# A zeroed tile multiplied with itself from the start of a two-block transformer kernel, and one modulation chunk moved behind the root

## What is computed

```python
c_act = jax.nn.silu(c)
for l in range(DEPTH):
    mod = c_act @ w_ada[l] + b_ada[l]
    sh1, sc1, g1, sh2, sc2, g2, sh3, sc3, g3 = jnp.split(mod, N_MOD, axis=-1)
    x = x + 0.5 * g1[:, None, :] * swiglu(modulate(x, sh1, sc1), ffn1_gate[l], ffn1_up[l], ffn1_down[l])
```

## Time and profile before

| | |
|---|---|
| median of 3 runs | 2202.4 us (2200.0 to 2204.21) |
| the profiled execution | 2208.11 us |
| its span, first to last instruction | 2206.3 us |
| mean granted TensorE clock over the span | 0.987 |
| TensorE busy | 2143.5 us, 97% |
| VectorE busy | 1525.2 us, 69% |
| ScalarE busy | 1170.7 us, 53% |
| HBM read | 418.81 MB |

### The profile page before, as it was taken

One profiled execution on the slowest core, in us unless ns is written; L12 is line 12 of the kernel. 1 busy time (PEld: TensorE's weight loads), 2 busy tenths in 40 slices (PEclk: granted clock), 3 DMA queues, 4 the chain that ended last, 5 costly groups with the idle time before them and its releaser, 6 DMA issues.

```text
span 2206.3 us, 40729 instructions
## 1 busy us (share of the span) xinstructions
PE 2143.5 (97%) x16760; PEld 1926.9 (87%) x16760; DVE 1525.2 (69%) x2118; ACT 1170.7 (53%) x2038; POOL 374.4 (17%) x357
## 2 busy tenths in 40 slices
PE   8999999999999999999999999999999988999998
PEld 5888988888888889899888999888878978898887
DVE  6897857688779867767775785476657544546754
ACT  4564457565555544674655565565446432446542
POOL 0141022111111110311111002210232440033001
PEclk9999999999999999999999999999998899999999
DMA  7987762567667867525665545355533300334552
GB/s 304 359 293 274 262 247 97 165 249 266 244 249 280 292 246 292 188 96 165 243 216 199 184 163 179 106 193 182 189 125 134 125 4 3 134 129 159 186 188 97
DMA packets 116824, 425.14 MB, mean 193 GB/s; under 512 B 12960, under 2 KB 14752, under 8 KB 115744
## 3 DMA queue, kind: packets, MB, share of 16 engines
q1 hardware_dynamic: 113040, 410.04, 53.1%
q10 hardware_dynamic: 3600, 12.49, 1.5%
HBM read 418.81 MB, written 3.67 MB: 191 GB/s over the span
## 4 chain that ended last, share of the span: by engine, by line
PE 84%; DVE 6%; issue 4%; ACT 4%; POOL 1%; DMA 1%; SPq 0%; DVEq 0%; ACTq 0%; POOLq 0%
PE banks L594 83%; DVE weight_lower L1689 1%; POOL heap L2983 1%; ACT weight_upper L2418 1%; PE banks L1128 1%; DMA weight_ring<-w_ada_row_dram 0%; PE banks L1509 0%; ACT xn_t L2596 0%; DVE xn_t L1910 0%; DVE heap L2029 0%; DVE heap L2183 0%; DVE xn_t L1907 0%; ACT heap L2629 0%; DVE silu L1904 0%; DVE heap L2095 0%
## 5 line engine op out<-in xcount | busy, mean ns | idle before, releaser
L1689 DVE TENSOR_TENSOR weight_lower<-weight_ring,weight_upper 128x1024 fp32r<-128x1024 f32 x580 | 743.0, 1288 | 281.6 <-ACT weight_upper L2418 280.0
L594 PE MATMUL banks<-xn_halves,weight_upper 128*128 128x512 f32 (+1 forms) x3680 | 809.8, 342 | 0.8 <-DVE xn_halves L2012 0.7
L2418 ACT ACTIVATE weight_upper<-weight_ring 128x1024 fp32r<-128x1024 f32 x580 | 607.2, 1053 | 292.7 <-PE banks L594 191.6
L594 PEld LDWEIGHTS banks<-xn_halves,weight_upper 128*128 128x128 f32 x3680 | 619.9, 190 | 63.2 <-issue 1.1
L594 PE MATMUL banks<-xn_halves,weight_lower 128*128 128x256 f32 x2832 | 526.4, 284 | 4.5 <-DVE xn_halves L1722 2.1
L594 PEld LDWEIGHTS banks<-xn_halves,weight_lower 128*128 128x128 f32 x2832 | 437.1, 191 | 28.7 <-DVE xn_halves L1722 3.2
L594 PE MATMUL banks<-hidden,weight_upper 128*128 128x512 f32 x1216 | 312.1, 395 | 0.6 <-DVE heap L2154 0.6
L2983 POOL TENSOR_TENSOR heap<-heap 128x256 f32<-128x256 f32 x120 | 122.0, 1021 | 891.8 <-ACT heap L2715 597.4
L594 PEld LDWEIGHTS banks<-hidden,weight_upper 128*128 128x128 f32 x1216 | 215.7, 188 | 39.9 <-DVE heap L2154 0.7
L1700 DVE CUSTOM_DVE_ANT_0 weight_ring<-weight_ring,c_rows,vecs 128x1024 f32<-128x1024 f32 x140 | 185.4, 1328 | 21.1 <-DMA weight_ring<-w_ada_dram 20.6
L594 PEld LDWEIGHTS banks<-hidden,weight_lower 128*128 128x128 f32 x1216 | 166.9, 188 | 16.0
(11 more groups left out here) (312 smaller groups left out, 2428.6 us busy)
## 6 DMA issues: line engine op xcount, KB each, us to landing
weight_ring<-w_ada_dram SPq DMA_DIRECT2D x140, 512.0 KB, 4.6
weight_ring<-ffn_gate_dram SPq DMA_DIRECT2D x88, 512.0 KB, 3.9
weight_ring<-ffn_up_dram SPq DMA_DIRECT2D x88, 512.0 KB, 4.5
weight_ring<-ffn_down_dram SPq DMA_DIRECT2D x88, 512.0 KB, 3.4
weight_ring<-m_w_up_dram SPq DMA_DIRECT2D x64, 512.0 KB, 3.7
weight_ring<-m_w_down_dram SPq DMA_DIRECT2D x64, 512.0 KB, 3.2
weight_ring<-w_in_dram SPq DMA_DIRECT2D x58, 512.0 KB, 4.0
weight_ring<-b_w_rkv_dram SPq DMA_DIRECT2D x24, 512.0 KB, 3.3
```

The source lines that it names most:

```text
L594: return nc.tensor.matmul(o, w, r, start=first, stop=last)
L1689: V.tensor_tensor(w_lo[:, n % RING, :], ring[:, n % RING, :], w_hi[:, j % SPLITS, :].bitcast(F32), ALU.subtract).then_inc(*did("weight_low ...
L2418: A.activation(w_hi[:, j % SPLITS, :], ring[:, n % RING, :], ACT.Copy).then_inc(*did("weight_upper", j))
```

## The change

`ADA_AHEAD` falls from 6 to 5, and the sixth chunk is worked behind the reciprocal of the root. A tile `blank` (128 x 128, in `work`) is zeroed by VectorE as its first instruction. TensorE waits for that and multiplies `blank` with itself 28 times into bank 2, then waits for the constants and for `c` as before. The identity is then multiplied 12 times instead of 8, and four further times between `shift_rows(0)` and `squares_sum`. The 28 products are in no way read.

```diff
-ADA_AHEAD = 6
+ADA_AHEAD = 5
@@
+        blank = work[:, 8 * S:8 * S + P]
@@
+            pe.wait_ge(*of("blank", 0))
+            for _ in range(28):
+                mm(cols(2, P), blank, blank, True, True)
             pe.wait_ge(*of("consts_in", 0))
             pe.wait_ge(*of("c_silu", 0))
-            hold(2, 8)
+            hold(2, 12)
             for k in range(BY_ROW):
                 ada_take(ADA_FIRST[2 * k:2 * k + 2])
                 if k == 1:
+                    hold(2, 4)
                     for j in range(KD):
                         squares_sum(0, j, KD)
                     spread(0)
@@
+            V.memset(blank, 0.0).then_inc(*did("blank", 0))
             bias_steps()
             modulated(*ADA_FIRST[:ADA_AHEAD])
             rstd(0)
+            modulated(ADA_FIRST[ADA_AHEAD])
             lv = vec("lam", 0, KD)
```

## The result

The changed kernel takes 2212.8 us in the median of 9 runs (2202.8 to 2216.0), the kernel before 2202.4 (9 runs, 2198.7 to 2206.2). The ratio is 1.0039, with a 95% interval from 1.0023 to 1.0055: 8.6 us slower, where 2.8 us faster was forecast, and outside the range. (The ratio goes by all runs of a set; the two medians alone are 10.4 us apart.) A second set gave 1.0043 (1.0027 to 1.0059).

The account below looks back on a forecast made before the run. TensorE, busy 97% of the span, was taken as the bound, so only time before the FFN counts. The VectorE chain's 2.5 us, 2.5 to 3.2 between medians, was taken as 2.8: 2202.4 - 2.8 = 2199.6 us, range 2197.0 to 2204.5.

Parts of the forecast that it names:

- The zeroed tile, row 0, the identities: TensorE's start: zeros raise the clock, ending at 9.2 to 10.1 us; row 0 takes 1.88 instead of 3.57 us.
- rival C: TensorE's start: products of zeros don't raise the clock, squares end 2.1 us later; 2205.3 us, chance 0.07.
- The squares: TensorE's 32 records of squares: 4.34 us instead of 6.99, so their end moves from 23.20 to 20.0 us.
- The chunk behind the root: VectorE at the root: moving the sixth chunk gives back 0.6 to 0.7 us and saves 0.15; VectorE chain gains 2.5.
- TensorE behind the root, and the transfers: Spreading to shift columns: clock costs 0 to 0.9 us, at most 0.2 shows; transfers 13 to 16 start earlier, stay covered.
- The sum at the start: Start up to the FFN: 2.5 us off the profiled execution, 2.5 to 3.2 between medians, 2.8 taken.
- The rest of the kernel: From 42.98 us on: TensorE is the bound and untouched, so the start's saving comes off the end, nothing more.
- D: Behind the start: a transfer-bound stretch takes the gain back, time stays at 2202.4 us; chance 0.12.
- Range and chances: Whole kernel: 2197.0 to 2204.5 us; 0.79 within 0.2%, 0.16 for faster and 0.05 for slower by more.

Follow-up runs that it names:

- e9: Changed kernel with its last 20 identity products before the FFN replaced by 34 tiny and 14 identity products (128 records over the kernel before): 2203.0 us, ratio 0.9996.
- e3: Changed kernel with six chunks ahead of the root as before (zeroed tile without the moved chunk): 2213.2 us, ratio 1.0048 to the kernel before.
- e13: e9, the changed kernel padded to a whole piece of code, run again unchanged: 2202.7 us, ratio 1.0006 to the kernel before.
- e15: e9, the padded changed kernel, with six chunks ahead of the root again instead of five: 2206.6 us, ratio 1.0029 to the kernel before.
- e16: Kernel before with 6 tiny products (12 records) added: 2206.1 us, ratio 1.0018.
- e5: Kernel before with 36 one-column products (72 records) added ahead of TensorE's wait for the constants: 2212.6 us, ratio 1.0049.

## Why the prediction was wrong, point by point

- *The zeroed tile, row 0, the identities.* Right. Start at 1.05 (1.0 expected), zeros end at 10.3 (9.2 to 10.1), so the clock rose slightly later than in both cases; row 0 at 12.97 for 1.88 us (12.7 to 12.9). Zeros raise the clock: rival C is out, since row 0 ran at the upper level in the changed kernel.
- *The squares.* Over-sized: 3.63 us in the first trace, under my lower bound of 3.8, for the 4.34 taken. Other executions of such kernels have 3.85 (e9), 4.08 (e3) and 4.32 (e13).
- *The chunk behind the root.* Wrong in sign at the start. I had it give back 0.6 to 0.7 us and save 0.15. With six ahead, the FFN begins 1.3 us later in the kernels without padding (41.35 against 40.08 and 39.98); with padding 42.13 lies between 40.83 and 42.41. What was wrong is the time at which the sixth chunk would be done: I took 20.52 from the trace of before, where nobody waited; with its transfer it was 19.70 + 1.28 = 20.98 (e15), with the root at 19.7. Nor does six give the upper parts a start: with its table load in between, the first is at 23.23 us in e3 and at 23.25 in the changed kernel. What is then late is TensorE's chain of rows, not VectorE's queue.
- *TensorE behind the root, and the transfers.* Right: row 1 took 3.35 us, mostly at the lower level, the shift columns ended at 31.77, and `first_shifts` came at 32.25 instead of 35.60 without waiting for them. SyncE's pause was 8.08 us instead of 11.73.
- *The sum at the start.* 3.4 us against the profiled execution, 2.5 forecast; 0.6 of the difference stands at the reciprocal already (19.80 for 20.4), by the quicker squares. But the reference was mis-sized: I called that execution the one with the quickest rise, and took other executions to be up to 0.9 us later. The traces of kernels whose start has no full products of zeros and no moved chunk put the first eight FFN products at 43.44, 41.63, 41.89, 41.81, 41.66, 41.64, 43.68 and 44.56 us. Their mean is 42.5, and in five of eight the squares already run at the upper level. Three of these five have 100 or 128 tiny records at their start, which may have helped; of the two traces of the kernel before itself, one is of either kind. The changed kernel's start gives 40.08, 39.98, 40.21 and 39.95, mean 40.1. So the gain of the start is 2.5 us on average. That it is near the 2.8 that I put between medians is luck: the reason I gave was another.
- *The rest of the kernel.* This is the step that failed: "the untouched remainder starts at 42.98 us", and what is saved ahead of it "comes off the end, and nothing more". The remainder was not untouched. It stood 72 records later in TensorE's program, and TensorE waited for pieces of that program at other and costlier places. None of my rivals had that; D had the gain taken back on the way, but by transfers and down to nothing at most. 8.6 us slower with 2.5 us saved at the start makes 11 us lost behind it. The compressions show 2 to 5 us of that directly (12.0 to 14.3 us against 9.8 to 10.8), partly as the longer stall and partly as dense products at the lower clock. From the first tiny record to the `heap` products of 64x128 behind the next 32, at 299.38 in the changed kernel and 299.00 before, it is 22.9 to 26.7 us in the four kernels with 72 records and 19.2 to 20.2 in the ten with 0 or 128 at this place: 4.7 us more on average. The mixer's stretch of small products takes 77.6 to 79.0 us in the four against 74.0 to 77.3, 3.2 us more on average, and of these 3.0 are "issue".
- *Range and chances.* The range was built of clock cases and transfers. It gave 0.05 to a loss of over 0.2%. The scatter was taken from three runs of before (4 us wide), where larger sets spread over 15 to 20 us. No case of it had a loss of this size.

**What stays open.** Some 3 of the 11 us are not located; the clock falls in other places differ from execution to execution, so single traces can't settle it. In six of the 18 traces, with and without added records, the clock is low already at the 8 dense records between the runs of tiny ones (0.50 from 279.9 us in the changed kernel); why isn't known. The losses of e15 (1.0029) and e16 (1.0018) have no shown cause. Nor can it be told whether the padded kernels keep any of the 2.5 us: their traces put the FFN at 40.83, 41.24 and 42.41, a mean of 41.5, 1.0 us ahead of the unfilled ones, and 1 us is less than their intervals tell.

## What to carry to other kernels

Instructions that do nothing still move everything behind them in their engine's program, and in stretches of very short instructions the border of a code piece can be a stall. Before crediting or blaming a small edit, compare it with a version that adds the same number of idle instructions, and with one that fills up to a whole piece. And a filler that brings up the clock is worth what it saves on average over executions: here the squares ran at the upper level without full products of zeros in five of eight traces, one of them of the unchanged kernel.

## What the runs showed of the hardware that was not expected

- TensorE's program arrives in pieces of about 128 products with their weight loads (256 instructions, 16.4 KB). 72 idle records at the start cost 0.49% (0.32 to 0.67), 128 cost nothing (0.9998, 0.9979 to 1.0017).
- A wait for such a piece ends 2.15 to 2.89 us after its packet starts on q8 (168 waits in 18 traces). How much of that shows depends on how much work TensorE has left: 0.46 us in the kernel before, 2.91 in e5.
- Behind a stall of over 1 us in the first compression the dense products ran at the lower clock in all six traces that have one: granted 0.50 from 286.7 us in the changed kernel (stall 1.05), 0.56 from 291.7 in e5 (2.91). That is no rule: in the mixer of the kernel before stalls of 1.07 and 1.61 us leave it at 1.00.
- Products of a zeroed tile raise TensorE's clock like any others: 56 records in 8.3 to 9.3 us in eight traces, where all at the lower level would be some 12.2 (estimate, 56 x 0.218).
- A tiny product of one column by one takes 1.94 / 72 = 0.027 us a record. Behind 68 of them the granted clock was 0.67 over the next 5.1 us in e13, and 1.00 in e9.
